# Out product's first half given out over the attention loop's steps, and a reordered index stage, in a three-layer kernel on one Trainium2 core

## The reference

```python
# first block (272 tokens with 16 meta tokens)
h = h + 0.5 * swiglu(rmsnorm(h, g1), ...)
u = rmsnorm(h, mix_norm) @ w_in          # queries, keys, values, latent c, index queries/keys/weights
o_a = diff_attention(...)                # 4 heads, two softmaxes each
score = einsum('bqh,bqhk->bqk', w, relu(dots * IDX_DIM ** -0.5)); _, sel = top_k(score, 64)
o_b = softmax attention over the selected latents
h = h + concat(o_a, o_b) @ w_out
h = h + 0.5 * swiglu(rmsnorm(h, g2), ...)
# second block, layers l = 0, 1
proj = rms_norm(x, norm1_g) @ w_in
ya = mla_mixer(...)                      # 8 heads, blocks of 128 queries
yb = stick_breaking_mixer(...)           # 4 heads
yc = pool_mixer(u, pool_w, pool_scale)   # windowed means, one product
x = x + concat([ya, yb, yc]) @ w_out
x = x + hier_moe(rms_norm(x, norm2_g))   # 32 experts, 2 per token
```

## Time and profile before

| | |
|---|---|
| median of 3 runs | 1253.92 us (1249.89 to 1254.57) |
| the profiled execution's own time | 1255.84 us |
| its span | 1254.0 us |
| PE busy | 1148.3 us (92%) |
| DVE / ACT busy | 519.0 us (41%) / 427.8 us (34%) |
| DMA | 322.73 MB, mean 257 GB/s |
| chain that ended last | PE 74%, DMA 18%, DVE 4% |

### The profile page before, as it was taken

The page is one execution under the profiler, slowest core; times in us unless marked ns, Lnnn a source line. Parts: engine busy times, 40 slices in busy tenths (PEclk is TensorE's granted clock), DMA queues, the critical chain, the costliest instruction groups (busy, mean ns, idle before and its releaser), DMA issues.

```text
span 1254.0 us, 18711 instructions
## 1 busy us (share of the span) xinstructions
PE 1148.3 (92%) x7870; PEld 882.5 (70%) x7870; DVE 519.0 (41%) x986; ACT 427.8 (34%) x764; POOL 38.7 (3%) x46
## 2 busy tenths in 40 slices
PE   8999999989999999999999899777699998997775
PEld 7999999977579999999867655333188675442221
DVE  5665546784634665545752310100067512110001
ACT  5433345443544534345453311101045522110001
POOL 0000000200010000000400000000031000000000
PEclk9999999999899999999989899888799898999887
DMA  9745542641304555453582599999977546999995
GB/s 366 288 169 172 185 148 101 241 154 68 135 34 172 197 173 199 172 199 135 202 357 79 190 422 422 423 423 422 422 322 309 211 166 276 422 422 421 422 423 232
DMA packets 45914, 322.73 MB, mean 257 GB/s; under 512 B 5384, under 2 KB 5640, under 8 KB 7808
## 3 DMA queue, kind: packets, MB, share of 16 engines
q1 hardware_dynamic: 44304, 314.71, 63.5%
q0 software_dynamic: 688, 3.69, 0.8%
q10 hardware_dynamic: 832, 3.05, 0.7%
HBM read 320.36 MB, written 3.16 MB: 258 GB/s over the span
## 4 chain that ended last, share of the span: by engine, by line
PE 74%; DMA 18%; DVE 4%; issue 1%; ACT 1%; SPq 1%; ACTq 0%; DVEq 0%
PE bank L1215 13%; PE bank L1217 13%; PE bank L1216 13%; DMA arena<-in_stream 9%; PE bank L1225 7%; PE bank L1738 5%; DMA G<-in_stream 4%; DMA ring<-in_stream 4%; PE bank L1717 4%; PE bank L1757 3%; PE bank L1279 2%; PE bank L1303 2%; PE bank L1269 2%; PE bank L1773 1%; PE bank L1767 1%
## 5 line engine op out<-in xcount | busy, mean ns | idle before, releaser
L1215 PE MATMUL bank<-r_hi,w_hi 128*128 128x272 f32 (+1 forms) x928 | 266.2, 287 | 0.0
L1217 PE MATMUL bank<-r_hi,w_lo 128*128 128x272 f32 (+1 forms) x928 | 265.7, 286 | 0.0
L1216 PE MATMUL bank<-r_lo,w_hi 128*128 128x272 f32 (+1 forms) x928 | 265.3, 286 | 0.0
L1871 DVE TENSOR_TENSOR w_lo<-ring,w_hi 128x2048 fp32r<-128x2048 f32 x65 | 148.9, 2292 | 129.2 <-ACT w_hi L837 129.2
L837 ACT ACTIVATE w_hi<-ring 128x2048 fp32r<-128x2048 f32 x65 | 124.5, 1917 | 207.9 <-PE bank L1217 207.9
L1215 PEld LDWEIGHTS bank<-r_hi,w_hi 128*128 128x128 f32 x928 | 176.3, 190 | 0.2
L1217 PEld LDWEIGHTS bank<-r_hi,w_lo 128*128 128x128 f32 x928 | 176.2, 190 | 0.0
L1216 PEld LDWEIGHTS bank<-r_lo,w_hi 128*128 128x128 f32 x928 | 175.8, 189 | 0.1
L2355 DVE TENSOR_TENSOR arena<-arena,bank 128x256 f32<-128x256 f32 x16 | 6.7, 421 | 236.5 <-ACT arena L1111 236.5
L1111 ACT ACTIVATE arena<-bank 128x256 f32<-128x256 f32 x16 | 6.1, 384 | 256.0 <-PE bank L1738 256.0
L1717 PEld LDWEIGHTS bank<-rstd,arena 128*128 128x128 f32 x512 | 67.6, 217 | 15.0 <-issue 15.0
(11 more groups left out here) (365 smaller groups left out, 1965.6 us busy)
## 6 DMA issues: line engine op xcount, KB each, us to landing
ring<-in_stream SPq DMA_DIRECT2D x153, 1024.0 KB, 5.0
arena<-in_stream SPq DMA_DIRECT2D x74, 1024.0 KB, 26.2
sm<-in_stream SPq DMA_DIRECT2D x18, 1024.0 KB, 26.2
G<-in_stream SPq DMA_DIRECT2D x10, 1024.0 KB, 25.9
w_ukv<-in_stream SPq DMA_DIRECT2D x10, 1024.0 KB, 26.1
xn<-in_stream SPq DMA_DIRECT2D x10, 1024.0 KB, 26.1
sq<-in_stream SPq DMA_DIRECT2D x10, 1024.0 KB, 26.4
mixT<-in_stream SPq DMA_DIRECT2D x8, 1024.0 KB, 26.3
```

Of the source, the lines that this page charges most:

```text
L1215: mm(dst, w_high, x_high, start=first, stop=False)
L1216: mm(dst, w_high, x_low, start=False, stop=False)
L1217: return mm(dst, w_low, x_high, start=False, stop=last)
L1871: V.tensor_tensor(w_lo[:, q % 2, :], chunk((A_FFN1, A_FFN2)[f] + q), w_hi[:, q % 2, :].bitcast(F32), ALU.subtract).then_inc(S("w_lo_ready" ...
```

## The change

It has two parts.

**Second block, both layers.** The scores of the attention loop move to banks 4 and 5, and the turned probabilities and the values of a unit share bank 6 or 7 (values in the upper 256 columns). Banks 0 to 3 thus belong to the out product from the start. Its first half's 32 matmuls (`beside`) are given out: two per step for 13 steps, then one per step for 6. A turn now waits until the values of the unit two back are saved (`o_saved`), where it waited for that unit's `aT_saved`. `pool_mix` goes from the 9th unit to the 2nd, and from bank 1 to bank 3. The first scores wait for the first saved stick-breaking head only, and not the turns for all four.

**First block.** `score` gets two tiles, one per block of queries. On DVE the second block's sum starts after two rounds of the first block's selection. On PE unit 12 goes ahead of the last four dots, unit 13 ahead of the row sum, and each of units 14 to 16 ahead of the latents that it stood behind. ACT's squares, saved latents and splits are put in another order.

```diff
-        score = carve("score", W0, 272)
-        rel = carve("rel", W0 + 272, 4, 272)
+        score = carve("score", W0, 2, 272)
+        rel = carve("rel", at["score"], 4, 272)
...
+        def score_bank(u, g, m):
+            return bank[4 + g % 2] if u["kind"] == "m" else bank[2 * (g % 2) + m]
+
+        def turn_bank(u, g):
+            return bank[6 + g % 2] if u["kind"] == "m" else bank[4 + g % 2]
+
+        def o_cols(u):
+            return 256 if u["kind"] == "m" else 0
...
-        POOL_AT = [SEG_M[l][0] + 8 for l in range(LAYERS)]
+        POOL_AT = [SEG_M[l][0] + 1 for l in range(LAYERS)]
+        BESIDE = [2] * 13 + [1] * 6
...
                 pe.wait_ge(S("probs_ready"), g + 1)
                 if g >= 2:
-                    pe.wait_ge(S("aT_saved"), g - 1)
+                    pe.wait_ge(S("o_saved" if u["kind"] == "m" else "aT_saved"), g - 1)
...
+            in_unit(12, 6, 0, T2)
             for h in range(4):
                 dots(12 + h)
-            in_unit(12, 6, 0, T2)
+            in_unit(13, 6, P, T2)
...
-                def turn_m(g):
-                    if g < SEG_M[l][0] + 2:
-                        pe.wait_ge(S("stick_saved"), SH * (l + 1))
-                    turn(g)
...
-                def first_half(g):
-                    if g == SEG_M[l][1] - 1:
-                        pe.wait_ge(S("scores_taken"), SEG_M[l][1])
+                def beside(n):
+
+                    c, f, d = n // 16, n // 8 % 2, n % 8
+                    if n % 16 == 0:
+                        loaded(pe, A_OUT2[l] + c)
+                    if n == 6:
                         pe.wait_ge(S("pool_saved"), 2 * (l + 1))
-                        down(A_OUT2[l], 0, 2, mixed, lambda k: [])
-
-                steps(SEG_M[l], (scores, 0), (pool_mix, 0), (first_half, 1), (turn_m, 2), (pv, 3))
+                    ins = mm(y_half(d), down_view(A_OUT2[l] + c)[:, f, P * d:P * d + P], mixed(2 * c + f),
+                             start=n < 8 and d % 2 == 0, stop=False, skip_group_check=True)
+                    if n % 16 == 15:
+                        ins.then_inc(S("down_used"), 1)
+
+                pe.wait_ge(S("stick_saved"), SH * l + 1)
+                g0, g1 = SEG_M[l]
+                n = 0
+                for j, count in enumerate(BESIDE):
+                    g = g0 + j
+                    if g < g1:
+                        scores(g)
+                        pool_mix(g)
+                    if j < 3:
+                        pe.wait_ge(S("stick_saved"), SH * l + min(j + 2, SH))
+                    beside(n)
+                    if 0 <= j - 2 < g1 - g0:
+                        turn(g - 2)
+                    if count == 2:
+                        beside(n + 1)
+                    n += count
+                    if j >= 3:
+                        pv(g - 3)
...
             take_top(0, 2)
             scale_first(10)
-            take_top(0, ROUNDS - 2)
-            select(0)
+            add_scores(1, 0)
             scale_first(11)
-            add_scores(1, 0)
+            take_top(0, 2)
+            scale_first(12)
             add_scores(1, 4)
             split_in(7)
-            scale_first(12)
-            take_top(1, 2)
             scale_first(13)
+            take_top(0, ROUNDS - 4)
+            select(0)
             split_in(8)
-            take_top(1, 2)
             scale_first(14)
-            take_top(1, 2)
+            take_top(1, 3)
```

More of the change, by code:

```diff
@@ L367, in build @@
         SQUARED1 = ["unit5", "unit6"]
+        SQUARED1 += ["unit12"]
         for t in range(4):
-            SQUARED1 += [f"unit{12 + t}", f"latent{2 * t}", f"latent{2 * t + 1}"]
-        SQUARED1 += [f"unit{16 + t}" for t in range(4)]
+            SQUARED1 += [f"unit{13 + t}", f"latent{2 * t}", f"latent{2 * t + 1}"]
+        SQUARED1 += [f"unit{17 + t}" for t in range(3)]
         FIRST_IN = KT
@@ L976, in _, with square_query, square_key @@
             act.dma_start(row_mat, row_consts).then_inc(S("rows_loaded"), 16)
-            for t in range(4):
+            def square_query(t):
                 square_unit(12 + t, sq[:, t, 0:T2], uT[:, t, NMETA:T1])
[L979 to L983, removed]
-                square_unit(16 + t, sq[:, 4 + t, :], uT[:, 4 + t, :])
-                if t in (0, 2):
-                    split_in(10 + t // 2)
+            def square_key(t):
+                square_unit(16 + t, sq[:, 4 + t, :], uT[:, 4 + t, :])
+            square_query(0)
+            square_query(1)
+            save_latent(0)
+            save_latent(1)
+            split_in(8)
+            square_query(2)
+            save_latent(2)
+            save_latent(3)
+            split_in(9)
+            square_query(3)
+            save_latent(4)
+            save_latent(5)
+            square_key(0)
+            save_latent(6)
+            save_latent(7)
+            split_in(10)
+            square_key(1)
+            square_key(2)
+            split_in(11)
+            square_key(3)
             def value_copy(dst, src, t):
@@ L1066, in save_pool @@
                         for t in range(2):
-                            nc.scalar.activation(mixT[:, 6 + t, 0:T2], bank[1][:, T2 * t:T2 * t + T2], ACT.Copy,
+                            nc.scalar.activation(mixT[:, 6 + t, 0:T2], bank[3][:, T2 * t:T2 * t + T2], ACT.Copy,
                                                  scale=gain(G_PS + 2 * l + t)).then_inc(S("pool_saved"), 1)
@@ L1417, in _ @@
                    skip_group_check=True)
[L1418 to L1423, removed]
+            first_saved(pe, 11)
+            latent(0)
+            latent(1)
+            in_unit(14, 7, 0, T2)
+            latent(2)
+            latent(3)
+            in_unit(15, 7, P, T2)
+            latent(4)
+            latent(5)
             for t in range(4):
                 in_unit(16 + t, 8 + t // 2, P * (t % 2), T1)
+                if t == 0:
+                    latent(6)
+                    latent(7)
                 first_squared(pe, "unit15")
@@ L1611, in _ @@
                 unit_free(pe, l, 16)
+                unit_free(pe, l, 17)
                 unit_free(pe, l, 18)
                 pe.wait_ge(S("k_rope_saved"), l + 1)
-                def turn_m(g):
-                    if g < SEG_M[l][0] + 2:
-                        pe.wait_ge(S("stick_saved"), SH * (l + 1))
-                    turn(g)
                 def pool_mix(g):
                     if g == POOL_AT[l]:
+                        unit_free(pe, l, 15)
                         pe.wait_ge(S("pool_d_ready"), 2 * l + 1)
                         for t in range(2):
-                            ins = mm(bank[1][:, T2 * t:T2 * t + T2], w_pool[:, t, :], pd[:, t, :], start=True, stop=True)
+                            ins = mm(bank[3][:, T2 * t:T2 * t + T2], w_pool[:, t, :], pd[:, t, :], start=True, stop=True)
                         ins.then_inc(S("pool_y_ready"), 1)
```

25 lines of the change are left out of this document (13 added, 12 removed).

## The result

The changed kernel takes **1235.95 us** (median of five runs; four lie at 1235.67 to 1236.81), against 1253.92 us before (five runs, 1249.89 to 1255.35). The ratio is 0.9868, with a 95% interval of 0.9839 to 0.9897: 18 us faster, where 17.2 were forecast.

A forecast was written before the change was run, and what follows sets the result against it. It took PE's holes and slow clock in the attention loops, and a PE hole in the first block, as what could be filled: 3.8 + 6.6 + 6.8 = 17.2 us off 1253.92, forecast 1236.5 us, range 1232 to 1242.

The forecast's parts named there:

- PE's sum: Second-block attention loop with 32 out-product matmuls inside: PE's work added up at full clock, 33.6 us per layer.
- Hand-over costs: Loop, switching between short and long matmuls: taken as 0, with bounds of 3.0 us lost or perhaps 1 us won.
- Rival A: Attention loops: the clock still falls for about 10 us per layer; won 7.0 us, time 1247 us; chance 0.11.
- Rival D: Both attention loops at slow clock throughout: 33.6 us become 67 each, time 1304 us, slower; chance 0.03.
- the loops' term: Attention loops of the two expert layers: 6.6 us won in the first and 6.8 us in the second.
- holes and slow clock are what can be filled: Old attention loop: PE's idle holes and 0.50 clock, not a wait for one engine, make up the time to win.
- 5.2 that can go: First block's projection: 3.22 us of PE standing before the row sum plus slow clock after it; 3.8 us won after new waits.
- the waits: First block, PE ahead of latent 4 and after one latent: 0.8 and 0.3 us, with other hand-overs 1.4 us lost.
- the clock's share: First block after the 3.22 us hole: about 0.8 us of the row sum and 1.2 us of two latents due to slow clock.
- the walk: First block, DVE's order of work step by step: unit 14 scaled at 268.2 us, so latent 4 comes late.
- Rival C: First block: its change gives nothing, DVE and ACT only trade one hole for others; time 1240.5 us; chance 0.09.
- Rival B: Expert stages: the weight stream hides the loops' gain, only the first block's 3.8 us is left; time 1250 us; chance 0.05.

The follow-up runs named there:

- the late one: Changed kernel with no out-product matmuls given out in the loop's first three steps and two in each of the other 16: 1239.26 us, ratio 0.9888.
- group 1: First set of follow-up runs, on one chip beside 22 runs of the kernel before (median 1249.77 us); the unedited changed kernel took 1238.32 us there, ratio 0.9896.
- part 2 alone: Kernel before with only the first block's new order and two score tiles, attention loops of the second block as before: 1245.26 us, ratio 0.9958.
- The parts alone: Two kernels, each the kernel before with one part changed: second-block loops only, 1240.56 us; first block only, 1245.26 us.
- the router's pause: Changed kernel with 13 unused 128-column matmuls ahead of PE's wait for the router's choice: 1237.81 us, ratio 0.9884.

## Why the prediction was right, and where it was not

- **The loop is PE's sum.** Forecast 33.6 us, measured 33.28 in ten loops of five profiles (all kernels with this giving out but the late one). Hand-over costs were taken as 0 and were 0.3 us better than that. Turns, values and scores wait for nothing.
- **The clock does not fall in the loop.** Rival A is refuted by 0 us of slow clock in every loop with work given out. The Trainium skill, page "TensorE: Matmul & The Clock Gate", section "A second HAM failure mode: psum-queue depth-cycling", tells of a PE that goes round the banks and stops briefly between groups, and whose clock falls again and again. Here PE goes round banks 0 to 7 in both loops and its clock stays at 1.00, but it has no such stops, so the page's case is not tested. Rival D goes with A.
- **The size of the loops' term was right for the wrong reason.** The sum took 40.2 and 40.7 us as what the old loop costs. That holds in three of the six profiled loops. One took 38.67, and two 36.5 to 37.0, where the change is worth 3.3 to 3.7 us. The step that failed is "holes and slow clock are what can be filled" as a fixed price: the two loops' term, forecast at 13.4 us, is 14.3 where the clock falls twice and 6.9 where it never does. In the one execution profiled then it had fallen twice, so the sum fitted that execution, and that is luck; that most of the runs timed beside it were such too is argued, not shown. Against before at 1249.8 (group 1) the same kernel wins 11.5 us, against 1253.9 it wins 18.
- **The first block.** Forecast 3.8, measured 4.28 at the loop's start. By the forecast's own terms, 5.2 that can go less the waits as measured, 1.06 instead of 1.4, make 4.1, and the waits' size explains most of the miss. The other terms are looser than that sum looks: the clock's share was put at 0.8 + 1.2 us, and the same rows got shorter by 0.48 (1.58 to 1.10) and 0.94 (2.07 to 1.13). The waits came in the place named and for the reason named; DVE had unit 14 scaled at 267.9 (267.48 and 0.42) where the walk had 268.2. Rival C is refuted by part 2 alone.
- **The weight stream hides nothing.** Rival B would have kept the full DMA stretch where it was; it starts 11.2 us earlier. The chance for it hung on the earlier trace rows, and they were the right rows: a share of 0.14 ahead of the stage, and an issue that waits for PE.
- **Together.** The parts alone add to 9.2 + 4.5 = 13.7 us, the whole on the same chip is 11.5. The intervals reach 3 to 5 us each way, so the parts add as far as can be told.

What stays open: from the first expert matmul of the last layer to the end, the profiles show 202.7 to 207.1 us for the same code, in no order that follows the edits, and the single traces differ from their medians by as much. Open too are what decides whether the clock falls behind the old hole, and what the branch behind the first gather spends its time on.

## What to carry to other kernels

Where an engine's row looks full at half clock, find the hole ahead of it: filling that hole, even with work for nothing, was worth 6 to 8 us here, and real work given out over it brought a further 3.5 us per loop by packing. Before an effect of the clock enters a sum, look at the same loop in every layer and in a second profile, since one profile shows a case and not the cost. A link made faster ahead of a stage gains only what the next link lets through, as the router's pause shows; and when two executions are compared in such a place, count from the start of the stage and not from the start of the span.

## What the runs showed of the hardware

The slow clock came or stayed away behind the same hole of the same code. Three-us stretches at the loop's start, columns as above, of the kernel before in its first profile

```profile
643.00:646.00 3.00, 1.63 (x10) 0.99 (x9) 2.47 (x17) 2.07 (x10) 0.00 (x0) 1.00 0.02 5
```

and in its second:

```profile
643.00:646.00 3.00, 1.69 (x9) 1.08 (x9) 2.52 (x18) 2.04 (x9) 0.00 (x0) 1.00 0.15 27
```

The first was followed by 10.2 us at 0.50 and the second by none. The hole is made of stops of 0.17, 0.79 and 0.41 us (the earlier trace rows show the last). The longest is this one, in the first profile:

```profile
644.72 0.30 PE L1290 MATMUL bank<-cst,arena 128*128 128x128 f32 x1 [0.79 <-issue]
```

Where the slow clock came in the attention loops of the expert layers it lasted 6.8 or 10.2 us, with PE fully busy in it. The Trainium skill, page "TensorE: Matmul & The Clock Gate", section "HAM oscillation", tells of a gap, a wait for DMA, that brings the slow clock on every time round the loop; here a hole whose longest stop is 0.79 us brought it in four of six loops.
